# Earlier token reads, a reordered router tail and norm rows by halves in a two-layer diffusion step

## What is computed

```python
for layer in range(2):
    h = modulate(rmsnorm(x), shift_a, scale_a)        # adaLN, from SiLU(cond) @ w_ada
    x = x + gate_a * (mla(h) if layer == 0 else neighbourhood_attention(h))
    h = modulate(rmsnorm(x), shift_f, scale_f)        # modulate: h * (1 + scale) + shift
    scores = sigmoid(h @ w_router)                    # 16 experts in 4 groups
    # biased scores: sum of the best two per group, best group, best two experts in it;
    # gate of an expert = its score / sum of both scores
    x = x + gate_f * sum over the token's 2 experts of
            gate_e * ((silu(h @ w_gate[e]) * (h @ w_up[e])) @ w_down[e])
y = rmsnorm(x)
```

## Time and profile before

| | us |
|---|---|
| median of 3 runs | 1468.11 (1463.69 to 1469.15) |
| the profiled execution's own time | 1466.69 |
| its span in the trace | 1464.9 |
| TensorE busy | 1277.3 |
| VectorE busy | 553.0 |
| ScalarE busy | 339.4 |
| GpSimd busy | 271.2 |

### The profile page before, as it was taken

The page is one execution under the profiler, slowest core; times in us unless marked ns, Lnnn a source line. Parts: engine busy times, 40 slices in busy tenths (PEclk is TensorE's granted clock), DMA queues, the critical chain, the costliest instruction groups (busy, mean ns, idle before and its releaser), DMA issues.

```text
span 1464.9 us, 18933 instructions
## 1 busy us (share of the span) xinstructions
PE 1277.3 (87%) x7270; PEld 737.8 (50%) x7270; DVE 553.0 (38%) x1417; ACT 339.4 (23%) x819; POOL 271.2 (19%) x362
## 2 busy tenths in 40 slices
PE   2899899999999679999819999999998886999990
PEld 2565466666645344444414455556774444444440
DVE  2221244444525644444401000004662565444442
ACT  3121244444412200000032000004662220001002
POOL 6110400010010062222120100113211003422221
PEclk9899999999999779999959999999999986999996
DMA  7622211131464759998750352243216236899955
GB/s 275 239 83 85 100 59 59 59 116 60 173 236 173 269 206 342 367 370 271 232 168 34 145 211 116 103 157 123 66 45 242 98 134 250 304 385 376 306 122 186
DMA packets 47765, 268.99 MB, mean 184 GB/s; under 512 B 9100, under 2 KB 15660, under 8 KB 33964
## 3 DMA queue, kind: packets, MB, share of 16 engines
q1 hardware_dynamic: 22588, 192.87, 34.1%
q0 software_dynamic: 19328, 53.93, 13.7%
q10 hardware_dynamic: 5760, 20.97, 3.6%
HBM read 231.28 MB, written 34.88 MB: 182 GB/s over the span
## 4 chain that ended last, share of the span: by engine, by line
PE 75%; DMA 10%; DVE 6%; issue 4%; ACT 4%; POOL 0%; ACTq 0%; POOLq 0%; DVEq 0%; PEldq 0%
PE PS L1070 14%; PE PS L816 12%; PE PS L1157 10%; PE PS L723 9%; PE PS L1029 8%; PE PS L1087 7%; PE PS L935 4%; DMA xrows<-big,info 3%; PE PS L735 3%; PE PS L966 2%; DMA big<-hrows,info 2%; DMA resid<-in_x 2%; PE PS L894 2%; DMA big<-in_const 1%; PE PS L976 1%
## 5 line engine op out<-in xcount | busy, mean ns | idle before, releaser
L723 PE MATMUL PS<-const,big 128*128 128x128 f32 (+2 forms) x643 | 98.6, 294 | 75.0 <-ACT big L1259 33.4
L723 PEld LDWEIGHTS PS<-const,big 128*128 128x128 f32 (+2 forms) x643 | 82.1, 150 | 122.2 <-issue 79.6
L1029 PE MATMUL PS<-weights,ht 128*128 128x512 f32 x320 | 142.1, 599 | 1.7 <-DVE ht L1551 1.6
L1157 PE MATMUL PS<-ht,weights 128*128 128x128 f32 (+1 forms) x512 | 140.2, 434 | 1.5 <-PE PS L735 0.9
L816 PE MATMUL PS<-weights,ht 128*128 128x336 f32 (+1 forms) x320 | 119.9, 533 | 5.9 <-DVE ht L1641 2.4
L1070 PE MATMUL PS<-big 128*128 128x512 f32 x256 | 116.5, 609 | 3.2 <-DVE big L1945 3.2
L1157 PEld LDWEIGHTS PS<-ht,weights 128*128 128x128 f32 x512 | 77.8, 191 | 64.1 <-issue 64.1
L1029 PEld LDWEIGHTS PS<-weights,ht 128*128 128x128 f32 x320 | 60.0, 192 | 71.6 <-issue 71.6
L520 POOL DMA_DIRECT2D modrows<-modrow x32 | 18.2, 572 | 396.7 <-DVE modrow L1551 280.1
L816 PEld LDWEIGHTS PS<-weights,ht 128*128 128x128 f32 x320 | 61.8, 196 | 58.2 <-issue 42.7
L1466 ACT ACTIVATE big<-PS 128x256 f32<-128x256 f32 x34 | 13.1, 385 | 331.4 <-PE PS L1070 331.4
(11 more groups left out here) (218 smaller groups left out, 1818.9 us busy)
## 6 DMA issues: line engine op xcount, KB each, us to landing
weights<-in_ada SPq DMA_DIRECT2D x24, 2048.0 KB, 8.6
big<-in_gu SPq DMA_DIRECT2D x16, 2048.0 KB, 13.2
weights<-in_gu SPq DMA_DIRECT2D x12, 2048.0 KB, 13.9
rows<-in_down SPq DMA_DIRECT2D x18, 1024.0 KB, 7.4
weights<-in_down SPq DMA_DIRECT2D x16, 1024.0 KB, 7.2
ht<-in_gu SPq DMA_DIRECT2D x6, 2048.0 KB, 13.7
weights<-in_qkv SPq DMA_DIRECT2D x6, 2048.0 KB, 11.8
weights<-in_wo SPq DMA_DIRECT2D x4, 2048.0 KB, 8.6
```

The lines of the kernel that those rows point to most:

```text
L723: return pe.transpose(dst, src, const[0:n, C_ID:C_ID + n])
L1029: ins = pe.matmul(bank(4 + j), OT[:, k, t * P:(t + 1) * P], w[j][:, k, :], start=(k == 0), stop=(k == KD - 1))
L1157: ins = pe.matmul(bank(bb, n1 - n0), w[:, k, m * P:(m + 1) * P], hT[:, k, n0:n1], start=(k == 0), stop=(k == KD - 1))
```

## The change

- In layer 1 SyncE waits for `r_ab` as well, before the loads of experts 0, 1 and 3.
- `h_rows` works in two halves of 512 columns, each multiply and add; `n_hd` counts twice per tile. Four of the transposes need the first half only.
- `logits` of a tile comes ahead of `counts`: for the last tile ahead of `counts(NT - 2)`, in the loop of layer 0 both come ahead of `ada(1, t)`.
- The last tile's right half of the columns is copied by ScalarE, and VectorE's `columns(NT - 1)` is gone from between `groups(NT - 2)` and `choose(NT - 2)`.
- Two of the 18 token reads are taken out of the row. In the loop columns 38 and 40 are read ahead of the gather, as soon as the add two before has landed, and GpSimd waits for both reads before the gather; behind the add no read is left. The last add gets a read of its own after the loop.
- ScalarE runs a dummy square root (`warm`) before it waits for the last adds.

```diff
@@ SyncE
                     sp.wait_ge(a_pv, 2 * NW)
                     sp.wait_ge(r_g, 32 * 3)
+                    sp.wait_ge(r_ab, 80 * 2)
                     load_gu(0)
...
-                sp.wait_ge(n_hd, hrow(f"f{l}", NT))
+                sp.wait_ge(n_hd, 2 * hrow(f"f{l}", NT))
@@ GpSimd
                 for j in range(2):
-                    n = STAT - 1 + j
-                    tokens_in(slice(n * P, (n + 1) * P), 38 + 2 * j, e_inf[l][1])
-                for j in range(2):
                     n = STAT + j
                     tokens_in(slice(n * P, (n + 1) * P), 34 + 2 * j, e_gt[l][j])
...
                     if n == 4:
-                        pool.wait_ge(e_inf[l][1], 16 * 15)
+                        pool.wait_ge(e_inf[l][1], 16 * 13)
...
                         tokens_in(rows, 30 + 2 * j, e_inf[l][j])
-                        pool.wait_ge(e_inf[l][j], i * 32 + (32, 256)[j])
+                        pool.wait_ge(e_ys[l][j], i * 16 + 16 * 7)
+                        pool.nop().then_inc(e_gate, 1)
+                        tokens_in(bass.ds(i * (2 * P) + (STAT - 1 + j) * P, P), 38 + 2 * j, e_inf[l][j])
+                        pool.wait_ge(e_inf[l][j], i * 32 + (48, 240)[j])
                         pool.wait_ge(e_tr[l], i * 2 + (STAT + 1 + j))
...
                         add_rows(38 + 2 * j, j)
-                        pool.wait_ge(e_ys[l][j], i * 16 + 16 * 8)
-                        pool.nop().then_inc(e_gate, 1)
-                        tokens_in(bass.ds(i * (2 * P) + (STAT + 1 + j) * P, P), 38 + 2 * j, e_inf[l][j])
+                pool.wait_ge(e_ys[l][0], trips * 16 + 16 * 7)
+                pool.nop().then_inc(e_gate, 1)
+                tokens_in(bass.ds(trips * (2 * P) + (STAT - 1) * P, P), 38, e_inf[l][0])
+                pool.wait_ge(e_inf[l][0], trips * 32 + 32)
                 pool.wait_ge(e_yd[l], trips * 2 + STAT)
                 pool.wait_ge(e_ys[l][1], trips * 16 + 16 * 7)
-                pool.wait_ge(e_inf[l][0], trips * 32 + 16)
@@ TensorE, x_transposes
                 if s[0] == "f":
-                    pe.wait_ge(n_hd, hrow(s, t + 1))
+                    pe.wait_ge(n_hd, 2 * hrow(s, t + 1) - 1)
...
                 for c in range(KD):
+                    if s[0] == "f" and c == 4:
+                        pe.wait_ge(n_hd, 2 * hrow(s, t + 1))
@@ TensorE, out_projection
                         logit_parts(l, t - 1)
-                    if l == 0 and t < 4:
-                        ada(1, t)
                     if t >= 2:
                         counts(l, t - 2)
                     if t:
                         logits(l, t - 1)
+                    if l == 0 and t < 4:
+                        ada(1, t)
...
                 logit_parts(l, NT - 1)
+                logits(l, NT - 1)
                 counts(l, NT - 2)
-                logits(l, NT - 1)
                 counts(l, NT - 1)
@@ ScalarE, f_stage
-                    act.wait_ge(n_hd, hrow(s, t + 1))
+                    act.wait_ge(n_hd, 2 * hrow(s, t + 1))
...
                 columns(NT - 1)
+                act.activation(hT[:, 4:8, (NT - 1) * P:], bank(1).rearrange("p (c n) -> p c n", c=4), ACT.Copy).then_inc(n_td, 1)
                 parts(NT - 1)
@@ ScalarE, moe
+                warm(ACT.Sqrt)
                 act.wait_ge(e_ys[l][0], trips * 16 + 16 * 8)
@@ VectorE, h_rows
-                    link(dve.scalar_tensor_tensor(out=HB[t], in0=x_(t), scalar=rs[:, t:t + 1], in1=row(t // CTX), op0=ALU.mult, op1=ALU.mult))
-                    tt(HB[t], HB[t], row(2 + t // CTX), ALU.add).then_inc(n_hd, 1)
+                    for j in range(2):
+                        n = slice(j * 512, (j + 1) * 512)
+                        link(dve.scalar_tensor_tensor(out=HB[t][:, n], in0=x_(t)[:, n], scalar=rs[:, t:t + 1], in1=row(t // CTX)[:, n],
+                                                      op0=ALU.mult, op1=ALU.mult))
+                        tt(HB[t][:, n], HB[t][:, n], row(2 + t // CTX)[:, n], ALU.add).then_inc(n_hd, 1)
@@ VectorE, f_stage
                 groups(NT - 2)
-                columns(NT - 1)
                 choose(NT - 2)
@@ VectorE, moe
-                        dve.wait_ge(e_inf[l][1], 16 * 15)
+                        dve.wait_ge(e_inf[l][1], 16 * 13)
```

## The result

| | kernel before | kernel after |
|---|---|---|
| median, us | 1468.63 | 1453.14 |
| range | 1463.69 to 1471.86 (4 runs) | 1450.58 to 1454.78 (4 runs) |
| span in the trace | 1464.9 | 1453.0 |

The change makes the kernel 15.5 us faster, ratio 0.9896 with a 95% interval of 0.9863 to 0.9929. The direction was forecast, the size was not: 24.5 us were promised, and 1453.14 lies just beyond the upper end of the range, 1453.

What follows compares the result with a forecast made beforehand. TensorE, busy for 87% of the span, was taken as the bound, so only work that makes it idle pays. Gains of 8.1 + 5.1 + 8.7 + 2.6 = 24.5 us gave 1443.5 us, range 1438 to 1453.

Steps and rivals of the forecast that it cites:

- 1. SyncE's wait: Layer 1's output projection: expert loads start behind the constants, so TensorE's 5.97 us stall goes whole; 8.1 us gained.
- the bound taken from layer 0: Landing of layer 1's router constants: at worst 12.9 us after issue, as the same transfer took beside a load.
- The prediction's estimate for all seven transfers of GpSimd together: Gate rows, modulation rows and router constants of layer 1, 3.4 MB: 9.7 us from 1111.3, landed at 1121.
- 2. The router's tail: Last tile of the router stage, both layers: halved h rows, earlier sum and ScalarE's copy gain 5.1 us.
- the term 2 x 2.8 = 5.6: Both layers: VectorE begins tile 4 2.8 us earlier, and everything to the first gather follows at its old distance.
- The loop: Router loop over tiles: the sum's wait for ScalarE's copy costs 0.5 us, once, in layer 0's tile 0.
- The risk that had been named, the store of h rows: First gather also waits for the last h rows' store, about 515, while wanting to start near 516.
- 3. The token reads: Adds at the experts' end: early reads bring the last add 5.8 us sooner in layer 0, 2.9 in layer 1; 8.7.
- So I take them as back at 732: Layer 0's token reads, in line behind the first add, return at 732, making the second add 4.8 us earlier.
- Rival B: Token reads don't stand in line behind the add; part 3 gives its high bound, 1439.5 to 1441 us; chance 0.12.
- Rival D: Adds are limited by their own landing, so early reads give nothing: 1452.2 us; chance 0.09.
- 4. The table load: Square-root table load before each layer's first norm moves into the add's wait: 2.6 us; 1.3 if x's later tiles land late.

Runs made afterwards that it cites:

- expert4_late: Kernel after, with the 2 MB load of expert 4's gate and up weights held until the second gather has landed: 1456.86 us, ratio 0.9928 to the kernel before.
- rows_wait_only: Kernel before with only SyncE's new wait in layer 1 added: 1460.88 us, ratio 0.9952 to the kernel before.
- reads_only: Kernel before with only the token reads of the adds moved ahead: 1462.26 us, ratio 0.9953 to the kernel before.
- root_table_only: Kernel before with only the dummy square root added: 1466.18 us, ratio 0.9990 to the kernel before.
- prefetch_late: Kernel after, with all but the first weight load for layer 1's attention held until layer 0's last add has landed: 1454.16 us, ratio 0.9890 to the kernel before.
- prefetch_after_x: Kernel after, with all but the first weight load for layer 1's attention held until x's last tile is read back: 1445.60 us, ratio 0.9852 to the kernel before.
- after_again: Kernel after, unchanged, measured again on another occasion: 1451.84 us, ratio 0.9882 to the kernel before.

## Why the prediction was right or wrong

**1. SyncE's wait.** Right in mechanism and size: 8.1 forecast, 8.3 in the trace, 7.0 to 7.9 timed alone. The landing was better than the bound taken from layer 0 (9.7 against 12.9), and what was late next was the product's end, as said. The prediction's estimate for all seven transfers of GpSimd together was too short, 9.7 us; they took about 12.9 (1110.56 to 1123.4), early enough all the same.

**2. The router's tail.** This is the step that failed: the term 2 x 2.8 = 5.6. It rests on "From there to the first gather everything follows at its old distance", which holds up to the gather's issue, 2.8 us. The prediction then let the gather's data move with its issue and didn't price its transfer. The earlier trace rows stop at the router; the next wait of TensorE, 5.15 us for the gather at 524.98, was in the trace of before as well, and it belongs to a transfer behind a backlog of weights, which ends about 27.5 us behind the last half of x in both kernels. expert4_late shows that backlog as the cause, since 2 MB less in front gives 4.1 and 4.9 us back. Of the 5.6 some 1.4 return, as the third gather, waited for by 0.77 and 0.32 us before, is now there in time. The loop cost 1.13 us where 0.5 was taken: 85.01 us in the four kernels with the old order (before, rows_wait_only, reads_only, root_table_only) and 86.1 in those with the new one. Tile 0 costs 0.7, of which 0.40 is the wait for ScalarE that was foreseen; tiles 1 and 2, taken as covered, cost 0.2 each without any wait for ScalarE, by the order of the products alone. In the two traces part 2 gains 0.2 us in all (1.4 in layer 0's tail, less 0.1 in layer 1's and 1.1 in the loop), timed alone 1.3, not distinguishable from none, where 5.1 were forecast. The risk that had been named, the store of h rows, was not what held it.

The Trainium skill (DMA: Bandwidth & Descriptors, "Queues, rings and completion order") says that a DMA engine takes turns between its queues, packet by packet. By that rule alone GpSimd's gather should have got a share of the engines from its issue on, though its packets are small beside those of the weights. The trace agrees only in part: from 523 on both queues are served, but in the 4 us before, with the gather already issued, no packet of it was moved. Why is open.

**3. The token reads.** Mechanism right, size of layer 0 too large: 3.6 for 5.8. The term that was mis-sized is "So I take them as back at 732": they came at 736.12, 3.3 us after the landing of the add was seen. prefetch_late and prefetch_after_x show why: with 2 MB of weights beside them instead of 6.4 they return at most 9.4 us after their issue instead of 16, the first add lands after 9.2 and 8.6 us instead of about 14, and the whole chain of adds shrinks to 19 or 20 us. It is a bandwidth neighbour that neither the old nor the new order of GpSimd removes. Layer 1, where there is no such neighbour, gave 2.5 for 2.9, with the second add held by VectorE's gate rows as forecast. Rival B is out: in layer 0 the read came after the add's landing. (The 6.05 us read as the price behind an add could not have told this alone: a load of 512 KB, `in_gfin`, stood in GpSimd's queue between that add and the read, at 1405.95.) Rival D, no gain from the reads, is out by reads_only.

**4. The table load.** Layer 0 gave 1.3 as forecast. In layer 1 it gave 0.5: x's third tile lands too late, which is the case of the low bound. In layer 0 the same five loads of x are in time.

**The sum.** Along TensorE's path of the two traces, before to after: +3.0 up to layer 0's router tail (1.9 of it ahead of everything the change touches, nearly all of that granted clock, and 1.1 of the loop), -1.4 in that tail, -5.2 to the start of layer 1, +2.9 of granted clock behind it, -8.3 at part 1, +0.1 in layer 1's tail, -3.0 at the end: -11.9, as the spans differ. The forecast had +0.5, -2.8, -7.1, 0, -8.1, -2.8, -4.2. Of the shortfall of 9 us (24.5 less 15.5), some 4.2 are the gathers, 0.6 the loop, 2.6 the adds, 0.8 the table; the last 0.8 is less than what the granted clock does from one execution to the next. The range was too narrow at its slow end because each of its bounds kept the gather as a fixed distance; all low bounds together gave 1451.4.

## What to carry to other kernels

A step moved ahead of a transfer is worth only what the transfer's landing moves: before counting it, look at what the DMA engines carry at the moment of issue, and ask whether the landing is set by the issue or by a backlog. When a long stretch is a chain of small dependent transfers (add, index read, add, read-back), keep bulk prefetches out of it to its very end if their consumers have slack; here about 6 us came from one wait on the prefetch's side (ratios 0.9896 and 0.9882 became 0.9852 and 0.9845), and the same wait ended at the wrong point gave nothing. Where every place in a stretch is crowded, postponing a load moves the collision and can make it worse, as the four kernels here with held expert weights showed.

## What the runs showed that was not expected

- A token read of 1 KB came back 16.2 us after its issue beside an add and weight loads (719.94 to 736.12), and in at most 8.8 behind the same add with the weights held back (721.99 to 730.77 in prefetch_after_x). In the first case it came back 3.3 us after the add ahead of it.
- In after_again the first add of layer 0 and the read behind it held GpSimd's next gather for 15.04 us, in prefetch_late for 7.64. The add itself landed after 14.6 and 9.2 us, and after 6.2 in layer 1, where hardly any weights stream. More than half of its time in layer 0 is the neighbour's.
- The same kernel had stretches at half speed in one execution and not in another (granted clock 0.72 against 1.00 from 788 to 794). The idle time of 2.15 us ahead of it stands in all fourteen traces, so it doesn't decide by itself. What goes with it is an earlier stretch: in the six traces where the first product of layer 1 (the one at 762.27 in the first trace of the kernel after, 9.00) took 8.69 us or more, the product behind the idle time takes 8.80; in the eight where it took 8.45 or less, 7.1. Why is open. Such differences are worth 1 to 3 us of a span, so a term of that size can't be read from two spans; it has to be read from the stretch in which it is made.
